# Delta rule with unscaled keys, and its solver's result turned on VectorE, in a two-layer GLA / gated delta / latent attention block

## Chip, cores, metric

One core of a Trainium2 chip runs the whole program. The metric is the device time of one execution in microseconds. Everything is float32.

## What is computed

Two layers work on 512 tokens (256 context, 256 latent) of width 1024. Each layer has three token mixers beside each other: gated linear attention, a gated delta rule in both directions, and latent attention. Only the delta rule is touched. Its definition, cut:

```
def l2norm(x):
    xf = x.astype(jnp.float32)
    return (xf * lax.rsqrt(jnp.sum(xf * xf, axis=-1, keepdims=True) + EPS)).astype(x.dtype)
...
def gdn_chunk_scan(q, k, v, g, beta, s0):
    '''Chunked gated delta rule: S_t = exp(g_t)(I - beta_t k_t k_t^T) S_{t-1} + beta_t k_t v_t^T,
    o_t = q_t S_t. q, k: (B, T, H, DK); v: (B, T, H, DV); g, beta: (B, T, H); s0: (B, H, DK, DV).'''
```

q, k and v come from one projection, a centred convolution of five taps and a SiLU; q and k are then divided by their length over the 128 elements of a head (`l2norm`). Inside a block of tokens the rule needs the inverse of a unit lower triangular matrix L, whose entries below the diagonal are beta times a decay times a product of two keys. There are 8 heads, two directions.

## The kernel before

**Order.** `schedule()` writes one list of items, the plan, such as `("d2", l, g, tt)` for layer l, pair of heads g and token tile tt. `settle()` moves each kind of item by the number of places that the hand-written table `AHEAD` gives it. Each engine then walks the plan from front to end and emits its share of every item; it never passes an item for another. An item waits, through semaphores, for the parts of other engines that it reads, and for the last reader of the PSUM bank that it gets. So the order in the plan is the order on each engine, and a late item holds back everything behind it on that engine. Weights come in over SyncE's queue in units of 1 MB into a ring.

**The delta rule in items.** The heads go in pairs g = 0 to 3. For a pair:
- `dqkv` j = 0 to 5 (q, q, k, k, v, v): projection on TensorE; a ScalarE copy, `cv` with five taps on VectorE (L2124, L2126), SiLU (`dsilu`, `dsil2`; VectorE L2132, L2144).
- `dnq`, `dn` for j = 0 to 3: lengths of q and k. ScalarE squares 128x512 (L1743), TensorE sums over the partitions with a matmul by ONES (bank<-RS,ONES), ScalarE makes the reciprocal root (L1518, L1519), VectorE scales the 512 columns (L2150).
- `d1`, `d2` per token tile: TensorE transposes the summed gates (K,WORK), VectorE makes the decays (L2156, four a tile), TensorE makes k by k and k by q (WORK, 128x128), VectorE multiplies (L2167, L2169, L2170).
- `dd`, `dt` per token tile: ScalarE gathers blocks of 32 x 32 (L1765), VectorE transposes (L2177), SyncE writes the blocks to DRAM (`LD`).
- `sol`: GpSimd loads the blocks (L1104) and the betas (`BD`, L1105) and inverts all 32x32 blocks at once in 31 steps of a multiply and an add (L1114, L1116).
- `dv`: GpSimd writes the result to DRAM (`XD`, L1123) and reads it back in another order (L1129); VectorE copies it (L2199) and transposes four times (L2202).
- `dx`, `dya`, `dyb`, `dx6`, `dy6`: TensorE joins the 32x32 inverses to 128x128 ones by small matmuls; `dx` is the first of them (matmuls of 32x32). Then the scan `sk`, `sq`, `st`, `su`, `sa` runs over the token tiles.

`head(l, g)` is d1, d2, dd, dt of the four tiles and then sol; `invert(l, g)` is dv to dy6. In `gdn()` the pair g = 2 has a placing of its own:

```
            elif g == 2:
                n = len(early) // 2
                out += qk + weave(head(l, 3), early[:n]) + weave(invert(l, g), kv, early[n:])
```

All of head 3 stands ahead of `dv` of pair 2. For g = 0 and 1 the inversion of g is woven with the head of g + 1.

On TensorE all matmuls have one line, L1153 (helper `mm`), and all transposes L1156 (`tr`).

## Time and profile before

| | before |
|---|---|
| median of 3 runs | 2183.26 us (2180.09 to 2183.82) |
| profiled execution, its own time | 2180.62 us |
| span of the trace | 2178.7 us |
| mean granted TensorE clock | 0.991 |
| TensorE busy | 2109.8 us, 97% |
| VectorE busy | 927.1 us, 43% |
| ScalarE busy | 841.6 us, 39% |
| GpSimd busy | 294.7 us, 14% |

The span is that of one execution, which was itself timed with 2180.62 us; what lies around it is 1.9 us. Busy shares are means over the whole program: an engine with a small share can still be the one that is waited for in one place. In the trace a float32 matmul of the program leaves two records.

### The profile page before, as it was taken

How to read it: one execution, taken by the hardware profiler on the slowest of the kernel's cores; microseconds unless marked ns; L12 is line 12 of the kernel's file. 1: busy time of each engine (PE TensorE's matmuls, PEld its weight loads, DVE VectorE, ACT ScalarE, POOL GpSimd, SP SyncE). 2: the span in 40 equal slices, each digit the busy share in tenths (PEclk: the TensorE clock that was granted, in tenths of full speed). 3: DMA queues.
4: the chain of work that ended last, by engine and by line, in shares of the span. 5: the costliest groups of instructions: out<-in, count | busy, mean ns of one | idle time of the engine just before them, and what ended most of it. 6: DMA issues, size and time to landing. Idle time of an engine off the chain costs nothing. (4 is left out here: it accounts for less than half of the span.)

```text
span 2178.7 us, 31299 instructions
## 1 busy us (share of the span) xinstructions
PE 2109.8 (97%) x10890; PEld 1439.6 (66%) x10890; DVE 927.1 (43%) x2293; ACT 841.6 (39%) x2203; POOL 294.7 (14%) x623
## 2 busy tenths in 40 slices
PE   8999999999989999999999999999989979999998
PEld 5667576656556886555674446776676668976687
DVE  3023554857563235443231111246677653343321
ACT  1223354645443234444231112246556443245420
POOL 1000006153350000000000000000632641000000
PEclk9999999999999999999999999999999999999999
DMA  8326303221311022111122332231422312332333
GB/s 271 105 73 195 118 22 109 65 68 43 100 40 49 26 88 79 60 50 44 63 77 78 116 99 101 77 100 41 134 79 74 97 55 78 108 100 85 112 129 122
DMA packets 192443, 192.31 MB, mean 88 GB/s; under 512 B 28943, under 2 KB 186467, under 8 KB 191779
## 3 DMA queue, kind: packets, MB, share of 16 engines
q1 hardware_dynamic: 186048, 171.08, 25.4%
q0 software_dynamic: 4672, 18.89, 2.8%
q8 instruction: 92, 1.51, 0.3%
q10 hardware_dynamic: 1571, 0.34, 0.1%
q14 instruction: 60, 0.49, 0.1%
HBM read 180.78 MB, written 9.50 MB: 87 GB/s over the span
## 5 line engine op out<-in xcount | busy, mean ns | idle before, releaser
L1153 PE MATMUL bank<-hT,ring 128*128 128x512 f32 (+2 forms) x1856 | 715.1, 533 | 5.6 <-ACT hT L1557 3.6
L1153 PEld LDWEIGHTS bank<-hT,ring 128*128 128x128 f32 (+1 forms) x1856 | 331.7, 189 | 257.1 <-issue 239.1
L1153 PE MATMUL bank<-ring,hT 128*128 128x256 f32 (+2 forms) x2112 | 449.8, 368 | 0.0
L1153 PE MATMUL bank<-WORK 128*128 128x128 f32 (+6 forms) x3056 | 392.0, 286 | 37.3 <-DVE O L2202 13.3
L1153 PEld LDWEIGHTS bank<-ring,hT 128*128 128x128 f32 x2112 | 380.4, 190 | 62.4 <-issue 17.2
L1153 PEld LDWEIGHTS bank<-WORK 128*128 128x128 f32 (+4 forms) x3056 | 320.5, 170 | 144.9 <-issue 123.3
L1153 PE MATMUL bank<-yT,ring 128*128 128x512 f32 (+1 forms) x768 | 270.2, 489 | 0.0
L1153 PEld LDWEIGHTS bank<-yT,ring 128*128 128x128 f32 x768 | 139.2, 191 | 78.7 <-issue 69.7
L2126 DVE SCALAR_TENSOR_TENSOR WORK<-WORK,CW 128x512 f32<-128x512 f32 (+1 forms) x192 | 142.1, 740 | 2.2
L1512 ACT ACTIVATE E<-bank 128x512 f32<-128x512 f32 (+1 forms) x84 | 45.0, 536 | 207.4 <-PE bank L1153 198.2
L1116 POOL TENSOR_TENSOR WORK<-WORK 128x126 f32<-128x126 f32 (+22 forms) x248 | 107.3, 432 | 19.4
L1141 POOL DMA_DIRECT2D yT<-xs x2 | 1.1, 547 | 800.7 <-DVE MT L2010 800.7
L1153 PE MATMUL bank<-ring,WORK 128*128 128x384 f32 (+1 forms) x272 | 108.4, 536 | 0.0
L1114 POOL TENSOR_TENSOR WORK<-WORK 128x126 f32<-128x126 f32 (+22 forms) x248 | 100.9, 407 | 19.5
L1156 PEld LDWEIGHTS bank<-K,WORK 128*128 128x128 f32 x634 | 78.3, 142 | 34.8 <-issue 25.2
L1524 ACT ACTIVATE WORK<-bank 128x128 f32<-128x128 f32 (+3 forms) x182 | 47.3, 272 | 135.2 <-PE bank L1153 134.9
L1156 PE MATMUL bank<-K,WORK 128*128 128x128 f32 x634 | 98.3, 279 | 0.2 <-DVE WORK L2314 0.2
L1153 PE MATMUL bank<-MT,ring 128*128 128x512 f32 (+1 forms) x256 | 83.7, 486 | 2.7 <-DVE MT L2010 2.7
L1153 PEld LDWEIGHTS bank<-ring,WORK 128*128 128x128 f32 x272 | 50.1, 190 | 38.0 <-issue 22.7
L1153 PEld LDWEIGHTS bank<-MT,ring 128*128 128x128 f32 x256 | 48.5, 190 | 37.2 <-issue 32.5
L2344 DVE TENSOR_REDUCE WORK<-bank 128x1 f32<-128x512 f32 (+1 forms) x48 | 28.9, 602 | 83.1 <-PE bank L1153 83.1
L1850 ACT ACTIVATE WORK<-bank,WORK 128x512 f32<-128x512 f32 (+1 forms) x48 | 29.6, 616 | 82.6 <-PE bank L1153 52.3
(215 smaller groups left out, 2009.6 us busy)
## 6 DMA issues: line engine op xcount, KB each, us to landing
ring<-in_w_in_dram SPq DMA_DIRECT2D x92, 1024.0 KB, 5.3
ring<-in_w_branch_dram SPq DMA_DIRECT2D x24, 1024.0 KB, 5.1
ring<-in_ada_w_dram SPq DMA_DIRECT2D x18, 1024.0 KB, 7.1
ring<-in_w_out_dram SPq DMA_DIRECT2D x8, 1024.0 KB, 5.1
WORK<-in_ada_w_dram SPq DMA_DIRECT2D x6, 1024.0 KB, 12.6
ring<-in_mla_q_up_dram SPq DMA_DIRECT2D x8, 576.0 KB, 4.1
xs<-yT POOLq DMA_DIRECT2D x2, 2048.0 KB, 7.5
WORK<-LD POOLq DMA_DIRECT2D x16, 256.0 KB, 3.4
```

Source lines behind the costliest of these rows:

```text
L1114: link(pool, "pool", pool.tensor_tensor(t, a[:, j + 1:BASE, j:j + 1].broadcast_to([P, m, w]), y[:, j:j + 1, 0:w].broadcast_to([P, m, w]), ...
L1116: ins = pool.tensor_tensor(y[:, j + 1:BASE, 0:w], y[:, j + 1:BASE, 0:w], t, ALU.subtract)
L1141: pool.dma_start(yT[:, :, :], xs[l]).then_inc(s_back, 16)
L1153: return nc.tensor.matmul(o, a, b, start=start, stop=stop, skip_group_check=True)
L1156: return nc.tensor.transpose(o, a, ident)
L1512: link(act, "act", nc.scalar.activation(dst, src, ACT.Abs))
L1524: ins = nc.scalar.activation(MT2[:, c0:c0 + w], ps[:, c0:c0 + w], ACT.Square, accum_out=mS[:, at + i:at + i + 1])
L1850: ins = nc.scalar.activation(PM[:, s, 0:nk], ps[:, 0:nk], ACT.Exp, bias=MST[:, nth(it, "act") % 8, 0:1], scale=MSCALE, accum_out=MST[:, nt ...
L2126: ins = V_.scalar_tensor_tensor(acc, src, wv, acc, ALU.mult, ALU.add)
L2344: ln(V_.tensor_reduce(MST[:, j, 2:3], ps[:, 0:nk], AX_X, ALU.max))
```

## The change

The keys are no longer divided by their length. `d2` takes the diagonal of k by k, already in PSUM, by a multiply with the identity and a sum over each row (L2145, L2146, VectorE; `KN8`). ScalarE makes reciprocal roots of 128x8 numbers once a pair, and at the last tile's `dt` VectorE works them into the betas (`KB`, turned into the solver's layout `SLB` by one transpose) and into the decays (`EGK`). Where a product still holds an unscaled key, the length is put in as a factor: in `dv` (`KF`, its inverse), and in the PSUM reads of `dx` and `dx6`, which were copies. `dnq` and `dn` remain for q alone. The betas no longer go through TensorE, ScalarE and DRAM (`BT`, `BD`). The solver stores its result with the two block indices exchanged, so that its inner step is 32 elements instead of 1 (a row of the result was contiguous, now a column is), and VectorE turns it by four transposes (L2208) and a multiply (L2210), so that `XD` with its write and its load is gone. The solver's areas are freed by `dv` of the pair before. `AHEAD` has new numbers, and the cut for a pair's early projections now lies at k's SiLU.

```diff
-        XD = nc.dram_tensor("XD", (1, SYSTEMS * BLOCK_D), F32, kind="Internal").ap()
-        BD = nc.dram_tensor("BD", (DEPTH, 4, TT, 4, P), F32, kind="Internal").ap()
...
-                if v[2] < 4:
+                if v[2] < 2:
                     tail += [("dnq",) + v, ("dn",) + v, ("v", "dn") + v]
...
-                n = rest.index(("v", "dn", l, g + 1, 3)) + 1
+                n = rest.index(("v", "dsil2", l, g + 1, 3)) + 1
...
-                    y = SLY[:, 0:BASE * BASE // 2].rearrange("q (i k) -> q i k", i=BASE)
+                    y = SLY[:, 0:BASE * half].rearrange("q (k i) -> q i k", i=BASE)
+                    pool.wait_ge(*done(("dg", l), "dve"))
                     if n:
-                        pool.wait_ge(s_xout, 16 * n)
+                        pool.wait_ge(*done(("dv", (n - 1) // 4, (n - 1) % 4), "dve"))
...
+                    for b in range(NBLK):
+                        pool.dma_start(SLA[b * BASE:(b + 1) * BASE, :], bc(systems(LD)[b:SYSTEMS:NBLK, :], 0, [2, half, BLOCK_D])
+                                       ).then_inc(s_lblk, 16)
+                    pool.wait_ge(s_kbeta, n + 1)
...
-                    pool.dma_start(XD[0, :].rearrange("(q x) -> q x", q=P), SLY[:, 0:BASE * BASE // 2]).then_inc(s_xout, 16)
-                    pool.wait_ge(s_xout, 16 * (n + 1))
...
+                    if tt == TT - 1:
+                        act.wait_ge(s_ksum, TT * (rounds(l, g) + 1))
+                        kn = KN8[:, :, 2 * g:2 * g + 2]
+                        rsqrt(kn, kn, 1.0).then_inc(s_knorm, 1)
...
                 elif k == "d2":
                     _, l, g, tt = it
-                    dve.wait_ge(*done(("d1", l, g, tt), "act"))
...
+                    diag = LTP[:, g % 2, tt, :].rearrange("p (h n) -> p h n", h=2)
+                    ln(V_.tensor_tensor(diag, ps[:, 0:256].rearrange("p (h n) -> p h n", h=2), bc(ident, 1, [P, 2, P]), ALU.mult))
+                    V_.tensor_reduce(KN8[:, tt, 2 * g:2 * g + 2], diag, AX_X, ALU.add).then_inc(s_ksum, 1)
+                    dve.wait_ge(s_ksum, TT * rounds(l, g) + tt + 1)
+                    dve.wait_ge(*done(("d1", l, g, tt), "act"))
...
                 elif k == "dt":
                     _, l, g, tt = it
+                    if tt == TT - 1:
+                        dve.wait_ge(s_knorm, rounds(l, g) + 1)
+                        dve.wait_ge(*done(("dg", l), "act"))
+                        if rounds(l, g):
+                            dve.wait_ge(*done(("sol", (rounds(l, g) - 1) // 4, (rounds(l, g) - 1) % 4), "pool"))
...
+                        V_.transpose(SLB[:, :, :].rearrange("p e i -> p (e i)"), KB[:, :, :, :, :].rearrange("p e o t u -> p (e o t u)")).then_inc(s_kbeta, 1)
...
                 elif k == "dv":
...
+                    ln(V_.reciprocal(KF[:, :, 2:4], KN8[:, :, 2 * g:2 * g + 2]))
...
-                    dve.wait_ge(s_land, 32 * (rounds(l, g) + 1))
-                    link(dve, "dve", V_.tensor_copy(LAND[:, :, :].rearrange("p s (u k h) -> p (s u) k h", k=BASE // 2, h=2),
-                                                    LANDR.rearrange("p (v h k) -> p v k h", h=2, k=BASE // 2)))
+                    dve.wait_ge(*done(("sol", l, g), "pool"))
+                    for b in range(4):
+                        ins = V_.transpose(LANDR[:, b * P:(b + 1) * P], SLY[:, b * P:(b + 1) * P])
+                    ln(ins)
+                    link(dve, "dve", V_.tensor_tensor(LAND[:, :, :].rearrange("p s (u k h) -> p (s u) k h", k=BASE // 2, h=2),
+                                                      LANDR.rearrange("p (k h v) -> p v k h", h=2, k=BASE // 2),
+                                                      KF[:, :, :].rearrange("p t u -> p (t u)").unsqueeze(2).unsqueeze(3).broadcast_to(
+                                                          [P, 4 * TT, BASE // 2, 2]), ALU.mult))
```

The order of the instructions, first on TensorE in layer 0 around the head of pair 3. RS,ONES are the sums of `dn`, hT,ring projections, K,WORK transposes of d1. Before:

```order
L1153 MATMUL bank<-RS,ONES 128x512
L1153 MATMUL bank<-hT,ring 128x512 x8
L1153 MATMUL bank<-RS,ONES 128x512
L1156 MATMUL bank<-K,WORK 128x128 x8
L1153 MATMUL bank<-WORK 128x128 x8
L1156 MATMUL bank<-K,WORK 128x128 x4
L1153 MATMUL bank<-yT,ring 128x512 x2
```

After:

```order
L1136 MATMUL bank<-RS,ONES 128x512
L1136 MATMUL bank<-hT,ring 128x512 x14
L1139 MATMUL bank<-K,WORK 128x128 x8
L1136 MATMUL bank<-WORK 128x128 x8
L1139 MATMUL bank<-K,WORK 128x128 x4
L1136 MATMUL bank<-yT,ring 128x512 x2
```

The last sum of k ahead of the transposes is gone, and the projections stand together; the last of q's remains.

On VectorE, same place, from the third tile's d2 to the end of `dv` of pair 2. Before:

```order
L2167 TENSOR_TENSOR WORK<-bank,SQ 128x512
L2169 TENSOR_TENSOR SQ<-bank,SQ 128x512
L2170 TENSOR_TENSOR WORK<-SQ 128x256
L2006 TENSOR_TENSOR MT<-bank,E 128x512
L2177 STREAM_TRANSPOSE WORK<-WORK 128x64 x2
L2199 COPY WORK<-WORK 128x512
L2202 STREAM_TRANSPOSE O<-WORK 128x128 x4
```

After, from the last tile's d2:

```order
L2145 TENSOR_TENSOR WORK<-bank,K 128x256
L2146 TENSOR_REDUCE WORK<-WORK 128x2
L2152 TENSOR_TENSOR WORK<-bank,SQ 128x512
L2154 TENSOR_TENSOR SQ<-bank,SQ 128x512
L2155 TENSOR_TENSOR WORK<-SQ 128x256
L1988 TENSOR_TENSOR MT<-bank,E 128x512
L2181 STREAM_TRANSPOSE WORK<-WORK 128x64
L2166 TENSOR_TENSOR WORK<-WORK 128x4x2 x2
L2169 TENSOR_TENSOR WORK<-WORK 128x4x2 x2
L2171 COPY WORK<-WORK 128x4x2
L2172 COPY WORK<-WORK 128x2x16
L2173 STREAM_TRANSPOSE WORK<-WORK 128x64
```

and from there to the same transposes:

```order
L2176 TENSOR_TENSOR WORK<-WORK 128x4x2 x2
L2181 STREAM_TRANSPOSE WORK<-WORK 128x64
L2197 RECIPROCAL WORK<-WORK 128x4x2
L2208 STREAM_TRANSPOSE WORK<-WORK 128x128 x4
L2210 TENSOR_TENSOR WORK<-WORK 128x512
L2215 STREAM_TRANSPOSE O<-WORK 128x128 x4
```

Two operations are added to every d2, nine small ones (L2166 to L2176) ahead of the last `dt`, and `dv` has a reciprocal, four transposes and a multiply where it had a copy.

On GpSimd, from one solve's end to the next one's first step. Before:

```order
L1116 TENSOR_TENSOR WORK<-WORK 128x16
L1123 DMA XD<-WORK 128x512
L1129 DMA WORK<-XD 128x16x16 x2
L1098 MEMSET WORK 128x512
L1104 DMA WORK<-LD 64x1024
L1105 DMA WORK<-BD 64x32
L1104 DMA WORK<-LD 64x1024
L1105 DMA WORK<-BD 64x32
L1107 TENSOR_TENSOR WORK<-WORK 128x1024
L1110 COPY WORK<-WORK 64x16 x2
L1114 TENSOR_TENSOR WORK<-WORK 128x31
```

After:

```order
L1111 TENSOR_TENSOR WORK<-WORK 128x16
L1093 MEMSET WORK 128x512
L1098 DMA WORK<-LD 32x1x1024 x4
L1102 TENSOR_TENSOR WORK<-WORK,K 128x16 x2
L1105 TENSOR_TENSOR WORK<-WORK 128x1024
L1109 TENSOR_TENSOR WORK<-WORK 128x31
```

The write and the two loads of XD and the loads of BD are gone; the same 256 KB of L blocks come in four loads instead of two.

## Rows read from the trace of the kernel before

**Rows 1.** The page: busy us (share of the span) and records of each engine

```profile
PE 2109.8 (97%) x10890; PEld 1439.6 (66%) x10890; DVE 927.1 (43%) x2293; ACT 841.6 (39%) x2203; POOL 294.7 (14%) x623
```

**Rows 2.** Windows (us from start): busy time of PE, PEld, DVE, ACT, POOL

```profile
250.00:660.00 410.00, 396.95 (x2241) 253.26 (x2240) 261.19 (x563) 207.93 (x448) 137.64 (x293) 1.00 0.22 63
660.00:1440.00 780.00, 774.83 (x3231) 490.21 (x3233) 231.22 (x641) 243.00 (x724) 7.45 (x13) 1.00 0.22 71
1440.00:1860.00 420.00, 392.67 (x2683) 291.14 (x2684) 262.55 (x612) 216.43 (x500) 139.49 (x294) 0.98 0.29 85
```

**Rows 3.** Waits of TensorE by releaser: us in total, times, longest

```profile
PE bank L1153 <- DVE O L2202: 13.3, 3, 6.2
PE bank L1153 <- DVE WORK L2150: 9.4, 5, 5.5
...
PE bank L1153 <- ACT RS L1743: 2.3, 4, 0.8
```

**Rows 4.** TensorE by form: records, busy us, mean ns

```profile
L1156 PE MATMUL bank<-K,WORK 128*16 128x128 f32 x8 | 1.2, 273 | 0.0
```

**Rows 5.** TensorE, layer 0, head 3 to dx of pair 2: start, length, wait

```profile
592.07 1.02 PE L1153 MATMUL bank<-RS,ONES 128*128 128x512 f32 x2
592.93 1.04 PE L1156 MATMUL bank<-K,WORK 128*128 128x128 f32 x8
595.43 2.02 PE L1153 MATMUL bank<-WORK 128*128 128x128 f32 x16 [1.46 <-DVE WORK L2150]
...
611.15 0.23 PE L1153 MATMUL bank<-WORK 32*32 32x32 f32 x1 [5.45 <-DVE O L2202]
```

**Rows 6.** VectorE, the same place

```profile
594.59 0.69 DVE L2150 SCALAR_TENSOR_TENSOR WORK<-WORK,RS 128x512 f32<-128x512 f32 x1 [2.43 <-ACT RS L1519]
595.20 2.15 DVE L2156 SCALAR_TENSOR_TENSOR SQ<-bank,WORK,K 128x128 f32<-128x128 f32 x8
...
609.47 0.24 DVE L2177 STREAM_TRANSPOSE WORK<-WORK 128x64 f32<-128x64 f32 x1 [0.58 <-ACT WORK L1765]
609.65 0.43 DVE L2199 COPY WORK<-WORK 128x512 f32<-128x512 f32 x1
```

**Rows 7.** TensorE, layer 1: waits at pairs 0, 2 and 3

```profile
1589.26 1.38 PE L1153 MATMUL bank<-WORK 128*128 128x128 f32 x5 [5.46 <-DVE WORK L2150]
...
1762.87 0.23 PE L1153 MATMUL bank<-WORK 32*32 32x32 f32 x1 [6.25 <-DVE O L2202]
...
1811.18 0.18 PE L1153 MATMUL bank<-WORK 32*32 32x32 f32 x1 [1.58 <-DVE O L2202]
```

**Rows 8.** VectorE, layer 1: dv of pair 0, last dt of pair 3

```profile
1587.18 0.43 DVE L2199 COPY WORK<-WORK 128x512 f32<-128x512 f32 x1 [4.40 <-DMA WORK<-XD]
1587.64 0.89 DVE L2202 STREAM_TRANSPOSE O<-WORK 128x128 f32<-128x128 f32 x4
...
1761.19 0.25 DVE L2177 STREAM_TRANSPOSE WORK<-WORK 128x64 f32<-128x64 f32 x1 [0.87 <-ACT WORK L1765]
```

**Rows 9.** GpSimd, layer 1: start and end of the solve of pair 0

```profile
1540.38 1.96 POOL L1107 TENSOR_TENSOR WORK<-WORK 128x1024 f32<-128x1024 f32 x1 [3.09 <-DMA WORK<-BD]
...
1576.84 0.62 POOL L1123 DMA_DIRECT2D XD<-WORK  x1 [0.30 <-POOL WORK L1116]
```

**Rows 10.** VectorE by form: count, busy us, mean ns

```profile
L2006 DVE TENSOR_TENSOR MT<-bank,E 128x256 f32<-128x256 f32 x8 | 3.3, 413 | 3.4 <-PE bank L1153 3.4
L2344 DVE TENSOR_REDUCE WORK<-bank 128x1 f32<-128x256 f32 x16 | 6.8, 423 | 16.9 <-PE bank L1153 16.9
L2041 DVE TENSOR_TENSOR WORK<-WORK 128x4 f32<-128x4 f32 x16 | 2.5, 158 | 0.0
```

**Rows 11.** GpSimd: first multiply by form; one step's add, 1 and 15 columns

```profile
L1107 POOL TENSOR_TENSOR WORK<-WORK 128x1024 f32<-128x1024 f32 x8 | 15.5, 1943 | 27.1 <-DMA WORK<-BD 27.1
345.21 0.26 POOL L1116 TENSOR_TENSOR WORK<-WORK 128x30 f32<-128x30 f32 x1
376.68 0.25 POOL L1116 TENSOR_TENSOR WORK<-WORK 128x30 f32<-128x30 f32 x1
```

More of the change, by code:

```diff
@@ L1026, in _ @@
             todo = [(where[last_use[replaced[u]]] if u in replaced else -1, 0, n, u) for n, u in enumerate(units)]
-            todo += [(where[it], 1, 0, it) for it in plan if it[0] in ("dg", "dt")]
+            todo += [(where[it], 1, 0, it) for it in plan if it[0] == "dt"]
             for at, (_, scratch, _, u) in enumerate(sorted(todo, key=lambda t: t[:3])):
@@ L1101, in _ @@
                         pool.wait_ge(*done(("sol", (n - 1) // 4, (n - 1) % 4), "pool"))
+                    for b in range(NBLK):
+                        pool.dma_start(SLA[b * BASE:(b + 1) * BASE, :], bc(systems(LD)[b:SYSTEMS:NBLK, :], 0, [2, half, BLOCK_D])
+                                       ).then_inc(s_lblk, 16)
+                    pool.wait_ge(s_kbeta, n + 1)
                     for odd in range(2):
[L1103 to L1110 removed]
+                        link(pool, "pool", pool.tensor_tensor(SLY[:, odd:BASE * half:BASE + 2], SLB[:, 1, odd:BASE:2],
+                                                              kc(C_ODD + odd, 1).broadcast_to([P, half]), ALU.mult))
+                    pool.wait_ge(s_lblk, 16 * NBLK * (n + 1))
+                    link(pool, "pool", pool.tensor_tensor(a, a, bc(SLB[:, 0, :], 2, [P, BASE, BASE]), ALU.mult))
                     for j in range(BASE - 1):
@@ L1321, in _ @@
                            GG[:, :, r * BH:(r + 1) * BH])
-                    mm(ps[:, 64:128], ONES[:, :], GG[:, :, :])
-                    for tt in range(TT):
-                        ins = tr(psum(it, 1)[0:16, tt * P:(tt + 1) * P],
-                                 BETA[:, tt, :])
+                    ins = mm(ps[:, 64:128], ONES[:, :], GG[:, :, :])
                 elif k == "dn":
@@ L1349, in _ @@
                     _, l, g, tt = it
-                    for j in (2, 3):
-                        pe.wait_ge(*done(("dn", l, g, j), "dve"))
-                    pe.wait_ge(*done(("dsil2", l, g, 5), "dve"))
+                    for j in range(2, 6):
+                        pe.wait_ge(*done(("dsil2", l, g, j), "dve"))
                     for j in range(4):
@@ L2217, in _ @@
                     _, l, g, n = it
+                    if ("sa", l, g, n - 1) in where:
+                        dve.wait_ge(*done(("sa", l, g, n - 1), "pe"))
                     for u in range(4):
@@ L2249, in _ @@
                         dve.wait_ge(*done(("su", l, g, n - 1), "dve"))
+                        if ("sq", l, g, n) in where:
+                            dve.wait_ge(*done(("sq", l, g, n), "pe"))
                         for u in range(4):
```

113 lines of the change are left out of this document (55 added, 58 removed).

## The prediction

> **What bounds the kernel now.** The page's first part comes first: TensorE is busy 2109.8 of 2178.7 us [rows 1], so nearly all of the time is TensorE's own, and a gain must take work or waits away from it. VectorE has 927.1 us of work, which looks harmless, but the windows show where it lies: in the two delta-rule stretches it is busy 261.19 of 410 us and 262.55 of 420 us, and only 231.22 of 780 us between them [rows 2]. TensorE idles about 13 us in the first of those stretches, 27 in the second and 5 between (window less busy time, same rows). The waits by releaser then say what for: 13.3 us on the transposes of `dv`, in 3 waits; 9.4 us on VectorE's scaling of keys, L2150, in 5; 2.3 us in 4 waits on the squares for lengths [rows 3], which stand, by their starts, at sums of k. These three are the waits that the change touches.
>
> The two timelines side by side show what such a wait is. In layer 0 TensorE starts the transposes for head 3 at 592.93, waits 1.46 us for VectorE's scaling of k, runs out of other work, and waits 5.45 us more until 611.15, where `dx` of pair 2 starts [rows 5]. VectorE meanwhile is not waiting: from 595.20 to 609.65 it works nearly without a gap through the decays of head 3, and only then comes to `dv` of pair 2 [rows 6]. The copy there has no wait before it, so the solver's result had long landed. This stall is VectorE's queue, not the DRAM path. The same stands in layer 1 at 1762.87, 6.25 us [rows 7]. The DRAM path is waited for in one place: layer 1, pair 0. The solver's last add ends at 1576.54 (the write to XD at 1576.84, less its 0.30 of wait [rows 9]), VectorE's copy begins at 1587.18 after 4.40 us idle for XD, its transposes end at 1587.64 + 0.89 = 1588.53 [rows 8]; the scaling of the next keys is queued behind them, and TensorE waits 5.46 us for it [rows 7].
>
> **The change, part by part.** All sums are against the profiled execution, 2180.6 us.
>
> *Lengths of k on TensorE.* 2 keys x 4 pairs x 2 layers = 16 sums by ONES go, all 512 wide (k is needed for all tokens in both layers). One takes from 592.07 to the next instruction's start at 592.93, 0.86 us [rows 5]: 16 x 0.86 = **-13.8**. The busy time of the pair of records is 1.02 us in the same row, but records overlap, so starts decide. Bounds -13 to -15. Their ScalarE and VectorE work (16 x 0.69 us of L2150 = 11.0 us of VectorE [rows 6]) goes too.
>
> *The betas' transposes* go: 8 records, 1.2 us [rows 4], **-1.0** by starts.
>
> *Waits on k's lengths.* The 2.3 us on squares vanish [rows 3]: **-2.3**. Of the 9.4 us in five waits on L2150, 5.46 [rows 7] and 1.46 [rows 5] are dealt with below; three are left with 2.5 us. The product k by k now needs only the SiLU. I take three quarters, as one of the three lies in pair 2's chain of layer 1: **-1.8**.
>
> *Pair 0 of layer 1.* Before: solver's end to the end of the transposes 1588.53 - 1576.54 = 12.0 us. After: four transposes 0.89 [rows 8], a 128x512 multiply 0.69 (as L2150's, with the same two inputs in SBUF [rows 6]), four transposes 0.89, with gaps 2.7. So 9.3 us less. Against it the solver starts later, because its input comes later: the head's four d2 gain 3.34 us (below), nine small operations at 158 ns 1.4, of which about 1.5 fill gaps in VectorE's waiting for ScalarE's gathers (of the kind of 0.58 and 0.87 us [rows 6, 8]): 3.2. And the solver reads with an inner step of 128 bytes. The nearest rows are two adds of 30 elements of one step form: 0.26 us as 30 rows of one element, step 64 bytes, and 0.25 us as two contiguous runs of 15 [rows 11]. 0.01 us in 30 elements, over the 5712 elements of a solve (2856 for each of multiply and add): 1.9 us. Net 9.3 - 3.2 - 1.9 = 4.2 us sooner, while TensorE itself arrives 0.86 sooner, the sum in front of it being gone: 5.46 shrinks by **-3.3**. Bounds: whole (-5.5) if the head's additions hide; nothing if the solver's stride costs 5 us or more.
>
> *Pair 3 of layer 1*: the wait of 1.58 us on `dv` [rows 7] is shorter than the 4.2 us: **-1.6**.
>
> *Pair 2 of both layers.* Here nothing is gained by the shorter path, since the result was there early; the chain that is waited for is VectorE's own, and it grows. Each d2 has a 128x256 multiply from PSUM (413 ns, L2006) and a sum over 128x256 (423 ns, L2344) [rows 10]: 4 x 0.84 = 3.34 us. Nine small ones at 158 ns (128x4, L2041) = 1.4, less the 0.58 and 0.87 us for which VectorE stood idle at that `dt` [rows 6, 8]. `dv` has a reciprocal (0.16), four transposes (0.89 [rows 8]) and a multiply (0.69) for a copy (0.43): 1.3. Together 5.5 in layer 0, 5.2 in layer 1. Against it, the chain starts sooner: before, it began 2.27 us after TensorE's transposes, behind k's scaling (595.20 - 592.93 [rows 5, 6]). Now it waits for the transposes and for the last SiLU of k. But the new order puts k's last projection four projection matmuls nearer to the transposes (some 13 us of TensorE's work ahead instead of 16, at the trace's 0.43 us of start to start for 128x512), so the SiLU comes about as late as it can. I take 0.6 us of start each; bounds 0 and 1.6. **+9.5**; bounds +7.5 to +11. This is the term that speaks against the change: TensorE has the same work in that stretch, so each VectorE microsecond is a TensorE one.
>
> *Other inversions* (pairs 0 and 1, both layers). The same 4.8 us a head and 1.3 us a `dv` fall among convolution taps that have slack of unknown size, and `dx` waits there are small now. VectorE adds in all 8 x (3.34 + 1.4 + 1.3) = 48.6 us less 11.0 = 37.6. Bounds: 0 (hidden behind projections) and 12 (each of four inversions late by half of 6). I take **+4**, nearer to nothing, since these stretches show no `dv` wait now.
>
> *At nothing:* the factors in the reads of `dx` and `dx6` (same width, copy to multiply), new waits of `sk` on the last `sa` and of `su` on `sq` (each reader stands ahead in TensorE's own order), one wider transpose, four loads of L instead of two plus two of betas on GpSimd's queue (it idles between solves), and fewer writes on SyncE's. SyncE's new wait for the solver's loads stands ahead of `dt`; behind it queue the weights, and were they late this would cost, but the loads are through before a solve's first multiply, and a solve lasts 36 us (1540.38 to 1576.54 [rows 9]) ahead of the next one's input. `AHEAD` moves fills about by a few places; the work between the last `dt` and `dx` on TensorE (the order's counts at the trace's durations) comes out within 3 us of before in each pair, so nothing, +-3.
>
> Sum: -13.8 - 1.0 - 2.3 - 1.8 - 3.3 - 1.6 + 9.5 + 4 = **-10.3**, so 2170.3 us. The runs' median lies 2.6 us above the profiled execution (2183.26 to 2180.62): **2173 us**.
>
> **A price that a page has.** The row gives 1.9 us a solve for the step of 128 bytes. The Trainium skill, "GPSIMD Engine Reference", in its section on performance pitfalls for Q7 kernels, says that reading SBUF with a step of over 8 bytes costs about half as much again per element. The trace does not agree for the pair of adds above, 0.26 against 0.25 us, though both are short. By the page's rule, worked with the row of 1943 ns for 1024 elements [rows 11], it would be 0.95 ns x 5712 = 5.4 us a solve, the gain at pair 0 of layer 1 would vanish, and the sum be about -7.
>
> **The rivals.**
>
> *A, the additions hide.* For it: VectorE is at 63% in these stretches [rows 2], and the chain may start 1.6 us sooner and find d2 waiting for ScalarE's exponentials anyway, so that the diagonal costs nothing (it is put ahead of that wait). Against: in rows 6 VectorE has no gap between 595.20 and 609. Then pair 2 costs +3 and the rest 0: -24 + 3 = -21, median about 2162. Chance 0.20.
>
> *B, VectorE's load eats the gain.* 37.6 us more work, and if 60% of it lands on TensorE (22.6 us in place of 13.5), the sum is -1, median 2182. For it: late taps are late keys, which are a late next head. Against: the stretches' waits are few. Chance 0.16.
>
> *C, the other side: the solver with its step is slow.* If a solve takes x us more than the 1.9, `dv` is late in turn: pair 0 of layer 1 at once, the others once their slack is gone, for which I choose 5, 8 and 13 us (in those pairs no `dv` wait stands in rows 7, so some slack is there, and none is as tight as this one): cost x + (x-5) + (x-8) + (x-13), each where positive. It cancels the 10.3 at x = 7.7 and is past no change by 4.4 us at x = 9.3, a solver of some 47 us in place of 36. For it: no row has an inner step of 128 bytes with a long inner run. Against: the 64-byte row. Chance 0.10: time 2188 to 2200. The page's rule (x = 3.5) belongs to the forecast's range.
>
> **Numbers.** Forecast 0.50, its own range 2166 to 2179; A 0.20, 2159 to 2165; B 0.16, 2179 to 2187; C 0.10; 0.04 for a larger gain. Leaving out C and the far end of A, the range is 2161 to 2185. What this measurement tells from no change is 0.2%, 4.4 us: 2178.9 to 2187.6. Faster 0.48 + 0.20 + 0.04 + 0.01 of B = 0.73; same 0.02 + 0.14 = 0.16; slower 0.10 + 0.01 = 0.11.
>
> **What would show it.** RS,ONES with 16 fewer matmuls, TensorE's busy time 14 to 15 us lower. Before pair 2's `dx` in layer 0 waits of 6.9 + 4.9 = 11.8 us in all, where they were 1.46 and 5.45; in layer 1 about 6.25 + 4.6 = 10.9 (A: no more than 8 in each). In VectorE's rows L2145 and L2146 at 0.41 and 0.42 us, 32 each. Layer 1, pair 0: wait 1 to 3 us. GpSimd's adds within 5% of before; wrong if they take half as much again. The forecast fails if the scattered waits on `cv` or SiLU grow, which I sized by choice.

## The result, and the profile after

| | before | after |
|---|---|---|
| median | 2182.79 us (5 runs) | 2189.88 us (5 runs, 2188.56 to 2191.79) |
| ratio | | 1.0037 (95%: 1.0025 to 1.0048) |
| span of the trace | 2178.7 us | 2187.3 us |
| mean granted clock | 0.991 | 0.985 |

I had forecast 2173 us, within 2161 to 2185, and gave "slower" a chance of 0.11. The kernel became 7.1 us slower: outside the range, and slower where I had forecast faster.

The page of the changed kernel, span and busy time (answers to [rows 1]):

```profile
span 2187.3 us, 31284 instructions
PE 2096.4 (96%) x10850; PEld 1436.4 (66%) x10850; DVE 962.9 (44%) x2455; ACT 816.8 (37%) x2169; POOL 307.6 (14%) x599
```

TensorE's work did go: 13.4 us less busy time. VectorE has 35.8 us more, as the sum had it (37.6). So TensorE stands idle 90.9 us where it was 68.9. The waits of TensorE by releaser say for what (answers to [rows 3]; "issue" is a wait for which the profile names no releaser):

```profile
PE bank L1136 <- DVE O L2215: 32.1, 6, 11.4
PE bank L1136 <- issue: 7.8, 6, 3.1
...
PE bank L1136 <- DVE WORK L2274: 4.8, 5, 1.3
PE bank L1136 <- DVE WORK L2219: 3.7, 3, 2.2
```

L2215 are the transposes at the end of `dv`: 13.3 us in 3 waits are now 32.1 in 6. The waits on the scaling and the squares of k (9.4 and 2.3 us) are gone as forecast. L2274 is VectorE's part of `su` in the scan, L2219 its read of `dx`. Leaving out the waits on `dv`, and in the kernel before also the 11.7 us on the lengths of k, TensorE's idle time rose from 43.9 to 58.8 us. These 14.9 us are waits for which my sum had no term. The timeline of TensorE has the large ones (answers to [rows 5, 7]):

```profile
398.61 0.18 PE L1136 MATMUL bank<-WORK 32*32 32x32 f32 x1 [2.50 <-DVE O L2215]
609.84 0.23 PE L1136 MATMUL bank<-WORK 32*32 32x32 f32 x1 [11.39 <-DVE O L2215]
1581.00 1.03 PE L1136 MATMUL bank<-WORK 128*128 128x128 f32 x4 [2.04 <-DVE WORK L2126]
1588.29 0.23 PE L1136 MATMUL bank<-WORK 32*32 32x32 f32 x1 [6.27 <-DVE O L2215]
1670.55 0.18 PE L1136 MATMUL bank<-WORK 32*32 32x32 f32 x1 [0.98 <-DVE O L2215]
1696.48 1.36 PE L1136 MATMUL bank<-WORK 128*128 128x128 f32 x8 [3.07 <-issue]
1772.98 0.23 PE L1136 MATMUL bank<-WORK 32*32 32x32 f32 x1 [10.17 <-DVE O L2215]
```

L2126 is the product of a SiLU on VectorE, here that of k. Pair 2 waits 11.39 and 10.17 us, where the prediction said 11.8 and 10.9. That term is right. Pair 0 of layer 1 waits 2.04 + 6.27 us, where the prediction said 2.2 in all.

For pair 0 of layer 1, GpSimd's rows show why. Start of the loads, first multiply, and on VectorE the first transpose of the result:

```profile
1536.87 2.38 POOL L1098 DMA_DIRECT2D WORK<-LD  x4 [18.26 <-issue]
1546.08 2.02 POOL L1105 TENSOR_TENSOR WORK<-WORK 128x1024 f32<-128x1024 f32 x1 [5.84 <-DMA WORK<-LD]
1585.29 0.89 DVE L2208 STREAM_TRANSPOSE WORK<-WORK 128x128 f32<-128x128 f32 x4 [3.52 <-POOL WORK L1111]
```

The first multiply began at 1540.38 before [rows 9]; it is 5.7 us later. Of that 1.6 us is the first issue (1536.87 against 1535.23, each on its own run's clock) and 4.1 us the load: 9.2 us from the first issue instead of 5.2. In the quieter second solve of layer 0 the load takes 8.5 us; these are the rows of the kernel before, then of the one after:

```profile
430.12 0.55 POOL L1104 DMA_DIRECT2D WORK<-LD  x1 [44.17 <-issue]
435.06 1.91 POOL L1107 TENSOR_TENSOR WORK<-WORK 128x1024 f32<-128x1024 f32 x1 [2.83 <-DMA WORK<-BD]
```

```profile
424.91 2.39 POOL L1098 DMA_DIRECT2D WORK<-LD  x4 [25.80 <-DMA LD<-WORK]
433.43 1.91 POOL L1105 TENSOR_TENSOR WORK<-WORK 128x1024 f32<-128x1024 f32 x1 [5.57 <-DMA WORK<-LD]
```

The steps of the solve themselves, by line, all 248 of each; before, then after:

```profile
L1116 POOL TENSOR_TENSOR WORK<-WORK 128x126 f32<-128x126 f32 (+22 forms) x248 | 107.3, 432 | 19.4
L1114 POOL TENSOR_TENSOR WORK<-WORK 128x126 f32<-128x126 f32 (+22 forms) x248 | 100.9, 407 | 19.5
```

```profile
L1109 POOL TENSOR_TENSOR WORK<-WORK 128x126 f32<-128x126 f32 (+22 forms) x248 | 121.4, 490 | 19.4
L1111 POOL TENSOR_TENSOR WORK<-WORK 128x126 f32<-128x126 f32 (+22 forms) x248 | 120.4, 485 | 19.4
```

33.6 us more in 8 solves, 4.2 us each; I had taken 1.9. The adds take 12% more, where the prediction named 5% as its sign, and the multiplies 20% more.

**The clock.** The windows around pair 2 of layer 0; first the kernel before, then after (columns as in [rows 2]; the value ahead of the DMA share is the granted clock):

```profile
606.00:612.00 6.00, 0.85 (x62) 0.88 (x64) 4.96 (x14) 3.77 (x12) 0.00 (x0) 0.90 0.14 22
612.00:618.00 6.00, 6.00 (x143) 4.17 (x134) 2.72 (x7) 1.87 (x6) 2.52 (x5) 0.81 0.38 96
```

```profile
598.00:604.00 6.00, 0.45 (x2) 0.00 (x0) 5.76 (x14) 3.00 (x8) 0.00 (x0) 0.80 0.08 12
604.00:610.00 6.00, 0.16 (x12) 0.20 (x16) 5.72 (x26) 1.89 (x6) 0.19 (x1) 0.50 0.15 23
610.00:616.00 6.00, 6.00 (x105) 3.40 (x101) 1.51 (x4) 1.76 (x5) 3.21 (x7) 0.57 0.26 72
```

While TensorE stands, its granted clock falls to 0.50, that is from 2.4 to 1.2 GHz, and TensorE's next work runs at 0.57 of full speed for 6 us: 2.6 us lost on top of the wait. In the kernel before it was 1.1 us in the window behind the wait (0.81). The same loss, TensorE's busy time times what its clock lacks of 1, is 16.3 us over the whole of the execution before and 19.6 after. Idle time is 68.9 and 90.9 us, and so work at full clock 2093.5 and 2076.8. That adds up: 16.7 us of work less, 22.0 of idle more and 3.3 of slow clock more are the 8.6 us between the two spans. The sum had 14.8 us of work less, and no term for the clock.

The 3.3 us are not pair 2's alone. Its two falls cost 5.8 us together before and 7.5 after. Four smaller ones are new, of 1.7 us each, behind waits of 1.7 to 3.1 us; this is one, behind the 3.07 us at 1696.48, where TensorE is busy all the time:

```profile
1697.00:1701.00 4.00, 4.00 (x19) 3.64 (x18) 1.66 (x4) 2.19 (x4) 1.32 (x4) 0.57 0.77 211
```

Against them stand smaller losses elsewhere, most of it in the first 60 us (4.8 us before, 1.6 after), long before the delta rule begins. So how much slow clock belongs to the change isn't sharp: 3.3 us over everything, 6.3 from 60 us on (11.3 to 17.6, by windows of 2 us).

**Where the idle time lies.** I cut both traces at the starts of `dx`. TensorE's idle time grew by 6.7 and 8.0 us in the stretches that end at pair 2's `dx` (6.9 to 13.6 in layer 0, 9.2 to 17.2 in layer 1), by 1.1 and 5.2 in those that end at pair 1's, and by 2.6 between layer 0's pair 3 and layer 1's pair 0. Of the 14.7 us ahead of pair 2, 8.4 are the two large waits (with the 1.46 before them counted in the kernel before); the rest, 4.1 us of it in layer 1, is in smaller waits, the 3.07 us at 1696.48 and 2.23 us for the read of `dx` among them.

### The profile page after: what moved, and what is told of

The parts are those of the page before. It is cut to its first block, busy times and chain, and to the rows that moved or that the text cites. A ratio compares the mean times of both kernels' runs of the same rounds, so it can differ in the third digit from the quotient of the medians.

```text
span 2187.3 us, 31284 instructions
## 1 busy us (share of the span) xinstructions
PE 2096.4 (96%) x10850; PEld 1436.4 (66%) x10850; DVE 962.9 (44%) x2455; ACT 816.8 (37%) x2169; POOL 307.6 (14%) x599
## 3 DMA queue, kind: packets, MB, share of 16 engines
q0 software_dynamic: 10176, 14.59, 2.0%
## 4 chain that ended last, share of the span: by engine, by line
PE 85%; DVE 5%; POOL 3%; issue 3%; ACT 2%; DMA 1%; ACTq 0%; DVEq 0%; SPq 0%; POOLq 0%
PE bank L1136 82%; PE bank L1139 3%; POOL WORK L1109 1%; POOL WORK L1111 1%; DVE SQ L2137 1%; DMA WORK<-LD 1%; DVE WORK L2108 0%; DVE SQ L2154 0%; DMA ring<-in_ada_w_dram 0%; DVE WORK L2210 0%; DVE WORK L2208 0%; DVE WORK L2152 0%; DVE WORK L2146 0%; DVE WORK L2145 0%; ACT WORK L1747 0%
## 5 line engine op out<-in xcount | busy, mean ns | idle before, releaser
L1136 PE MATMUL bank<-WORK 128*128 128x128 f32 (+6 forms) x3056 | 393.9, 287 | 55.0 <-DVE O L2215 32.1
L1136 PEld LDWEIGHTS bank<-ring,hT 128*128 128x128 f32 x2112 | 380.5, 190 | 62.5 <-issue 16.7
L1109 POOL TENSOR_TENSOR WORK<-WORK 128x126 f32<-128x126 f32 (+22 forms) x248 | 121.4, 490 | 19.4
L1111 POOL TENSOR_TENSOR WORK<-WORK 128x126 f32<-128x126 f32 (+22 forms) x248 | 120.4, 485 | 19.4
L2010 DVE SCALAR_TENSOR_TENSOR WORK<-bank,WORK 128x512 f32<-128x512 f32 x16 | 11.1, 692 | 119.8 <-ACT WORK L1493 119.8
```

The lines of the kernel that those rows point to most:

```text
L1109: link(pool, "pool", pool.tensor_tensor(t, a[:, j + 1:BASE, j:j + 1].broadcast_to([P, m, w]), y[:, j:j + 1, 0:w].broadcast_to([P, m, w]), ...
L1111: ins = pool.tensor_tensor(y[:, j + 1:BASE, 0:w], y[:, j + 1:BASE, 0:w], t, ALU.subtract)
L1136: return nc.tensor.matmul(o, a, b, start=start, stop=stop, skip_group_check=True)
L2010: ins = V_.scalar_tensor_tensor(LA[:, tt, :], ps[:, :], 0.0, LT1, ALU.min, ALU.subtract)
```

## The experiments

Two theories at the start. **S**: the solver's result comes late (slower loads, slower steps) and that is the loss. **V**: VectorE's additions are the loss. `nodiag` and `nokn` leave out work that the result needs. The ratios are to the kernel before, timed beside each run. The changed kernel was timed in one session, so "faster than the changed kernel" compares medians of different sessions, in which the kernel before moved between 2181.66 and 2182.79 us: I don't tell differences of under 2 us apart.

**rows**: the result row by row again, read with a step by the transposes.

```diff
-                    y = SLY[:, 0:BASE * half].rearrange("q (k i) -> q i k", i=BASE)
+                    y = SLY[:, 0:BASE * half].rearrange("q (i k) -> q i k", i=BASE)
...
-                        ins = V_.transpose(LANDR[:, b * P:(b + 1) * P], SLY[:, b * P:(b + 1) * P])
+                        ins = V_.transpose(LANDR[:, b * P:(b + 1) * P].rearrange("p (k v) -> p k v", v=BASE),
+                                           SLY[:, 0:BASE * BASE // 2].rearrange("p (i k) -> p k i", i=BASE)[:, 4 * b:4 * b + 4, :])
```

> The changed kernel, but the solver keeps its result row by row (inner step 1 element, as before) and VectorE's four transposes read it with a step. Theory S (the loss is the solver's result coming late: slower loads and slower steps): a solve falls back by 3 to 4 us to about 33 us, the wait before dx of pair 0 in layer 1 falls from 6.3 to about 3 us, those of 2.5, 1.0 and 0.8 us go, the two waits of pair 2 (11.4 and 10.2 us) stay, and the time falls by 5 to 8 us against the changed kernel, ratio to before 1.000 to 1.0015. Theory V (VectorE's additions for the diagonal alone make the loss): under 2 us, ratio 1.003 to 1.004. VectorE's transposes with a step may cost more than 0.89 us; at twice that 1 us is given back.

Measured: 2186.37 us, ratio 1.0024 (1.0014 to 1.0033), 3.5 us faster than the changed kernel. Steps and transposes by line:

```profile
L1111 POOL TENSOR_TENSOR WORK<-WORK 128x126 f32<-128x126 f32 (+22 forms) x248 | 107.2, 432 | 19.4
L1109 POOL TENSOR_TENSOR WORK<-WORK 128x126 f32<-128x126 f32 (+22 forms) x248 | 104.8, 423 | 19.4
L2208 DVE STREAM_TRANSPOSE WORK<-WORK 128x128 f32<-128x128 f32 x32 | 9.6, 359 | 1.8 <-POOL WORK L1111 1.6
```

241.8 us of steps became 212.0: the inner step of 128 bytes costs 29.8 / 8 = 3.7 us a solve, 0.65 ns an element. The transposes pay 0.3 us a solve. The wait ahead of pair 0's `dx` in layer 1 is shorter, but 5.0 us and not the 3 that S gave, with 0.80 on L2126 where it was 2.04:

```profile
1586.71 0.23 PE L1136 MATMUL bank<-WORK 32*32 32x32 f32 x1 [4.98 <-DVE O L2216]
```

The waits of 2.50 and 0.98 us, which S said would go, are 2.76 and 1.31: longer by what the transposes pay, so there it is VectorE's own chain that is late, not the solver's result. Pair 2 waits 11.70 and 10.50 us. The time lies between the two theories' numbers. The slower step carries up to half of the loss (3.5 of 7.1 us, or 2.8 if each kernel is taken against the kernel before of its own session); the slower loads are not in it.

**load8**: eight loads of 16 rows in place of four that each copy 16 rows twice.

```diff
-                    for b in range(NBLK):
-                        pool.dma_start(SLA[b * BASE:(b + 1) * BASE, :], bc(systems(LD)[b:SYSTEMS:NBLK, :], 0, [2, half, BLOCK_D])
-                                       ).then_inc(s_lblk, 16)
+                    for b in range(2 * NBLK):
+                        pool.dma_start(SLA[b * half:(b + 1) * half, :], systems(LD)[b // 2:SYSTEMS:NBLK, :]).then_inc(s_lblk, 16)
```

> The changed kernel with eight loads of 16 rows for the blocks of L in place of four loads that each copy 16 rows twice. If the copying twice in one load is what cuts them into packets of 512 bytes, GpSimd's queue shows packets of 4 KB again (some 130 instead of 1088 per solve) and the time from the first issue to the first multiply is 8 issues of 0.6 us and then 2.9, 7.7 us, against 8.5 now and 5.0 before. If the rows' distance in DRAM is what cuts them, it stays over 8.5.

GpSimd's queue over the whole program, in the changed kernel, then here (packets, MB, share of 16 engines):

```profile
q0 software_dynamic: 10176, 14.59, 2.0%
```

```profile
q0 software_dynamic: 3520, 14.56, 2.0%
```

The same bytes in a third of the packets: the double copy in one load is what cut the rows. A solve's loads are 256 packets instead of 1088, twice the 130 that I had expected. The load now takes 6.4 us in layer 0's second solve (426.95 to 433.31), 2.1 less than in the changed kernel and less than the 7.7 expected. The kernel was executed once, with 2193.84 us, and pair 0 of layer 1 waits 6.18 us there, as in the changed kernel (6.27). One execution can't tell 2 us, so what the faster load is worth stays open.

**nodiag**: the diagonal's product and sum left out, the lengths a constant.

```diff
-                    ln(V_.tensor_tensor(diag, ps[:, 0:256].rearrange("p (h n) -> p h n", h=2), bc(ident, 1, [P, 2, P]), ALU.mult))
-                    V_.tensor_reduce(KN8[:, tt, 2 * g:2 * g + 2], diag, AX_X, ALU.add).then_inc(s_ksum, 1)
+                    V_.memset(KN8[:, tt, 2 * g:2 * g + 2], 1e4).then_inc(s_ksum, 1)
```

> The changed kernel without the diagonal: the multiply with the identity and the row sum in d2 are left out and the lengths set to a constant. Theory V: 4 x 0.84 = 3.3 us less at each head, 11.4 and 10.2 at pair 2 become about 8 and 7, and with pair 0 and 1 the time falls by 8 to 12 us, ratio to before about 0.999. Theory S: pair 2 gives 6.7 us and the clock some more, pair 0 of layer 1 gives up to 3 because the solver starts sooner: also 8 to 10 us. What tells them apart is where: under S the wait at pair 0 of layer 1 stays above 2 us.

Measured: 2170.01 us, ratio 0.995 (0.9938 to 0.9963), 19.9 us faster than the changed kernel. More than either theory had. The 26.7 us of VectorE work cost 19.9. (The constant that stands in their place takes 1.9 us of VectorE; from one start to the next a tile's part shrinks from 0.90 to 0.11 us, 25 us in all.) TensorE's waits:

```profile
PE bank L1136 <- DVE O L2213: 24.1, 5, 8.3
PE bank L1136 <- issue: 6.3, 8, 1.6
```

The time from one pair's dx to the next one's shrinks in layer 1 by 8.0 us ahead of pair 2, 2.0 ahead of pair 1, and 2.6 us between layer 0's pair 3 and layer 1's pair 0; in layer 0 by 5.8 and 1.5. It isn't pair 2 alone, though 13.8 of the 19.9 us are ahead of its `dx`, where four of the eight heads lie, with 13.4 us of diagonal; the two large waits shrink by 5.3. Between the two profiled executions, 14.4 us of idle time went, 8.0 of it on `dv` and 6.4 elsewhere, and 2.1 us of slow clock.

What was to tell the theories apart does not speak for V alone. At pair 0 of layer 1 the wait stays above S's 2 us, with 1.65 us on L2126 ahead of it:

```profile
1581.62 0.23 PE L1136 MATMUL bank<-WORK 32*32 32x32 f32 x1 [4.44 <-DVE O L2213]
```

So at that place the later result is a cause of its own, beside the diagonal.

**nokn**: the kernel before, k's lengths cut to 8 of 512 columns.

```diff
-                    a0 = q0 if it[3] < 2 else 0
+                    a0 = q0 if it[3] < 2 else T - 8
                     ins = mm(ps[:, a0:T], ONES[:, :], bSQ[:, a0:T])
```

> The kernel before, with the lengths of k cut from 512 to 8 columns (squares, sum, root and scaling of the other 504 left out; all SiLU products scaled by 0.01), nothing put in their place. This is the gain side of the change alone. My prediction's terms: 13.8 less a rest for 8 columns (16 x about 0.1), 2.3 and 1.8 of waits, and pair 2's waits of 6.9 shorter by about 0.6 each: 17 us, about 2165, ratio 0.992. If the removed work had been hidden or its place taken by other waits (theory H), under 8 us, ratio above 0.9965.

Measured: 2166.3 us, ratio 0.9931 (0.9918 to 0.9945), 15.7 us faster than before. The gain side of the forecast holds. Theory H falls. So what the change adds costs 2189.9 - 2166.3 = 23.6 us, net of what its shorter path to `dx` and its new order gain, and the diagonal with 19.9 is most of it.

**accum**: two multiplies that sum as they write, per tile.

```diff
-                    ln(V_.tensor_tensor(diag, ps[:, 0:256].rearrange("p (h n) -> p h n", h=2), bc(ident, 1, [P, 2, P]), ALU.mult))
-                    V_.tensor_reduce(KN8[:, tt, 2 * g:2 * g + 2], diag, AX_X, ALU.add).then_inc(s_ksum, 1)
+                    V_.scalar_tensor_tensor(diag[:, 0, :], ps[:, 0:P], 1.0, ident, ALU.mult, ALU.mult,
+                                            accum_out=KN8[:, tt, 2 * g:2 * g + 1])
...
```

> The changed kernel, with the diagonal's multiply and sum (128x256 each, 0.41 + 0.42 us) done by two 128x128 multiplies that sum as they write. Theory V2 (VectorE sets the pace of the heads' stretches, and some three quarters of its added time shows: 26.7 us of diagonal gave 19.9 us): at 0.27 us each (the multiplies of 128x128 by form) 32 x 0.3 = 9.6 us of VectorE less, time 6 to 8 us less, about 2183, ratio 1.000. Theory P2 (only the chain in front of pair 2's dx counts, the rest hides): 2 x 1.2 = 2.4 us less, ratio 1.0025. If the summing form is slower than 0.27 us, less of both.

Measured: 2181.25 us, ratio 1.0003 (0.9994 to 1.0011), 8.6 us faster. By form a multiply takes 0.28 us and the reading of its sum 0.08 more:

```profile
L2147 DVE SCALAR_TENSOR_TENSOR WORK<-bank,K 128x128 f32<-128x128 f32 x32 | 9.1, 284 | 0.0
L2147 DVE DVE_READ_ACCUMULATOR WORK<-bank,K 128x1 f32 x32 | 2.6, 82 | 0.0
```

By these records the diagonal's own work is 23.3 us instead of 26.7, and the time fell by more than that. But the records overlap. From the first start to the start of the next operation it is 0.90 us in the changed kernel and 0.54 here; first the changed kernel:

```profile
599.10 0.41 DVE L2145 TENSOR_TENSOR WORK<-bank,K 128x256 f32<-128x256 f32 x1
...
600.00 0.69 DVE L2152 TENSOR_TENSOR WORK<-bank,SQ 128x512 f32<-128x512 f32 x1
```

```profile
595.62 0.28 DVE L2145 SCALAR_TENSOR_TENSOR WORK<-bank,K 128x128 f32<-128x128 f32 x1
...
596.16 0.69 DVE L2154 TENSOR_TENSOR WORK<-bank,SQ 128x512 f32<-128x512 f32 x1
```

At 32 tiles that is 11.5 us of VectorE's queue less, and 8.6 us of time (7.5 if each kernel is taken against the kernel before of its own session) is 65 to 75% of it, near nodiag's 79% by the same count (19.9 of 25). P2 with its 2.4 us falls; V2 holds.

**oldorder**: seven numbers of AHEAD back to those of before.

```diff
-AHEAD = {... 'yT': 2, 'muk': -2, 'muq': 5, 'z2': 4, 'sk': 2, 'dsilu': 2, 'su': 1 ...}
+AHEAD = {... 'yT': -1, 'muk': -6, 'muq': 2, 'z2': -4, 'sk': -1, 'dsilu': -2 ...}
```

> The changed kernel with seven of the fifteen changed numbers of the order table set back to before's (sk, su, yT, z2, muk, muq, dsilu). Theory O (the new order is part of the loss: su behind sk's wait shows 1.3 us waits that were 0.4): 3 us or more faster, ratio 1.002 or less. Theory V2: the order was made for the changed kernel and moves little, within 2 us, or slower.

Measured: 2200.04 us, ratio 1.008 (1.0066 to 1.0094), 10.2 us slower. Theory O falls: the new numbers are worth 10 us to the changed kernel. What they would do to the kernel before was not tried.

**woven2**: pair 2 woven as pairs 0 and 1.

```diff
-                out += qk + weave(head(l, 3), early[:n]) + weave(invert(l, g), kv, early[n:])
+                out += qk + weave(weave(invert(l, g), kv), head(l, 3), early, phase=(-1.0,))
```

> The changed kernel with the inversion of pair 2 woven with the head of pair 3, as it is for pairs 0 and 1, in place of behind it. Theory P2: the waits of 11.4 and 10.2 us before dx of pair 2 fall under 2 us each, some of it comes back as waits inside the inversion, net 8 us or more faster, and the two falls of the granted clock (0.5 for 5 to 10 us) go: ratio under 1.000. Theory V2: the waits go from dx to the pieces of the head and to k by k, since VectorE has the same work in that stretch: 0 to 5 us faster from the clock and from the better filling. The solve of pair 3 starts later by some 3 us, which has to fit in the 9 us between its end and dx of pair 3.

Measured: 2203.31 us, ratio 1.010 (1.0086 to 1.0114), 13.4 us slower; both theories wrong in sign. The waits ahead of pair 2's dx are gone, and these stand ahead of pair 3's, in layers 0 and 1:

```profile
668.06 0.23 PE L1136 MATMUL bank<-WORK 32*32 32x32 f32 x1 [10.98 <-DVE O L2215]
1833.91 0.23 PE L1136 MATMUL bank<-WORK 32*32 32x32 f32 x1 [14.96 <-DVE O L2215]
```

The solve of pair 3 began at 629.50 in layer 0 where it was 618.50, 11 us later and not the 3 I had reckoned, and ended some 3 us ahead of that dx. Three microseconds are what `dv` takes, so it is now the solve that this `dx` waits for. P2, by which only the chain ahead of pair 2 counts, falls: the wait at pair 2 is the price of an early solve of pair 3.

**rows_acc_woven**: those three edits together.

> The changed kernel with three things: result stored row by row (-3.5 us alone), diagonal by summing multiplies, pair 2 woven. If they add: V2 gives -3.5 - 7 - 0 to 5, 2175 to 2179, ratio 0.996 to 0.998, faster than before; P2 gives -3.5 - 2.4 - 8 = 2176.

Measured: 2186.76 us, ratio 1.0026 (1.0017 to 1.0035). 3.5 + 8.6 - 13.4 would be 1.3 us slower than the changed kernel; it is 3.1 faster. They don't simply add.

**late**: the diagonal read once a head out of the 32x32 blocks that ScalarE gathers, where the decay is 1; the roots behind the last gather instead of ahead of it, the betas two items later. The two operations in each `d2` are gone; of the edit, this is what takes their place.

```diff
+                        cut = DC[:, 1, 0:TT * 2 * BASE].rearrange("p (t u i) -> p t u i", t=TT, u=2)
+                        ln(V_.tensor_tensor(cut, STG[:, :, 0:2 * BASE].rearrange("p t (u i) -> p t u i", u=2),
+                                            kc(C_SUM, 32).unsqueeze(1).unsqueeze(1).broadcast_to([P, TT, 2, BASE]), ALU.mult))
+                        V_.tensor_reduce(KN8[:, :, 2 * g:2 * g + 2], cut, AX_X, ALU.add).then_inc(s_ksum, 1)
+                        pending = [l, g, 0]
...
```

> The changed kernel, but the lengths are read from the 32x32 diagonal blocks that ScalarE has gathered anyway: once a head a 128x256 multiply and a 128x256 sum behind the last gather, in place of four of each in d2, and the nine small operations on the betas come two items later, while the solver's input is loading. The decay on the diagonal is 1, so the numbers are the same. VectorE loses 26.7 - 6.7 = 20 us. Theory V2 (three quarters of VectorE's time in these stretches shows): 15 us faster than the changed kernel, about 2175, ratio 0.996 to 0.9975. Theory S (the solver's lateness is what is left): under 8 us, ratio above 1.000. The betas must not come later than the load (7.9 to 9.2 us), or the solver waits for them.

Measured: 2182.28 us, ratio 1.0001 (0.9992 to 1.001), 7.6 us faster, half of what V2 said. ScalarE's timeline in layer 1, pair 2, shows waits that may hold the rest (the last row is the copy for the scan's first step):

```profile
1682.68 0.30 ACT L1498 ACTIVATE WORK<-WORK,EPSC 128x8 f32<-128x8 f32 x1 [1.86 <-DVE WORK L2191]
...
1684.30 0.58 ACT L1697 ACTIVATE WORK<-bank 128x512 f32<-128x512 f32 x1
...
1688.76 0.63 ACT L1711 ACTIVATE WORK<-WORK 128x512 f32<-128x512 f32 x1 [2.04 <-DVE WORK L2142]
1689.30 0.58 ACT L1789 ACTIVATE WORK<-bank 128x512 f32<-128x512 f32 x1
```

ScalarE waits 1.86 us for the sum, VectorE then 2.26 us for ScalarE's copy of v's projection (L1697), ScalarE 2.04 us for VectorE's SiLU, and TensorE stands 4.42 us, put down to issue; I take it to be for the scan's copy at the end of that queue. The first of these waits is new. In the changed kernel the roots stand ahead of the last gather, and their sums are there already:

```profile
1688.15 0.30 ACT L1497 ACTIVATE WORK<-WORK,EPSC 128x8 f32<-128x8 f32 x1
```

**late_rows**: late and rows.

> The same with the solver's result stored row by row (-3.5 us alone). If the two add, 2171, ratio 0.994 to 0.996; if the solver's lateness no longer matters once the heads are early (or matters more), the difference to the run above is 0 (or 5).

Measured: 2179.41 us, ratio 0.9987 (0.9978 to 0.9996). They add to 0.6 us.

**late_rows_dv**: and `dv` of pair 2 ahead of head 3.

```diff
+                out += qk + [("dv", l, g)] + weave(head(l, 3), early[:n]) + weave(invert(l, g)[1:], kv, early[n:])
```

> The same with dv of pair 2 placed ahead of the head of pair 3, and dx to dy6 where they were. The solver's result is there some 35 us before, so VectorE can turn it in a gap ahead of the head: 2.9 us less in each of the two chains that TensorE waits for, and a shorter fall of the clock: 4 to 7 us faster than without it. If VectorE has no gap there, no change.

Measured: 2181.3 us, ratio 0.9994 (0.9986 to 1.0003); no gain, 1.9 us slower by the medians. The wait moved from `dx` to its successor, for VectorE's read of `dx` (18.3 us in 3, the longest 8.8). The transposes of `dv` were only the place of the wait, not its cause.

**late2_rows**: late_rows with the roots two items later on ScalarE, the betas four on VectorE.

```diff
-LAG = 2
+LAG = 4
+ALAG = 2
...
+                if roots:
+                    roots[2] += 1
+                    if roots[2] > ALAG or (k in ("dd", "sol") and it[2] != roots[1]):
```

> As late_rows, but ScalarE takes the reciprocal roots two items after the last gather and VectorE the betas four items later, so that neither stands waiting for the other in front of v's convolution and of the scan's first copy. Theory Q (ScalarE's and VectorE's hand-over in the head's tail costs 1.9 and 2.3 us of standing in layer 1, pair 2, and the like elsewhere): 3 to 6 us faster than late_rows, 2174 to 2177. If the tail is VectorE's work and not its waits: no change.

Measured: 2169.45 us, ratio **0.9944** (0.9931 to 0.9958): 12.3 us faster than the kernel before, 20.4 faster than the changed one. It is 10.0 us faster than late_rows, where Q had 3 to 6. Between the two profiled executions TensorE's idle time fell by 5.8 us (80.5 to 74.7), which is Q's size, and the loss by slow clock by 7.7 (22.9 to 15.3), which Q had not; 3.1 of the latter lie in the first 60 us, where the edit does nothing. ScalarE in the same place:

```profile
1674.59 0.30 ACT L1499 ACTIVATE WORK<-WORK,EPSC 128x8 f32<-128x8 f32 x1
...
1677.73 0.63 ACT L1721 ACTIVATE WORK<-WORK 128x512 f32<-128x512 f32 x1 [0.76 <-DVE WORK L2150]
1678.27 0.58 ACT L1797 ACTIVATE WORK<-bank 128x512 f32<-128x512 f32 x1
```

The roots no longer wait. TensorE's waits put down to issue fall from 12.8 in late_rows to 5.9 us, those on `dv` stay (24.2 there):

```profile
PE bank L1138 <- DVE O L2235: 24.5, 5, 8.6
PE bank L1138 <- issue: 5.9, 6, 2.1
```

**late2_rows_st**: and `st` two places earlier (`'st': 2`).

> The same with the item st (the scan's first product and ScalarE's copy of it) two places earlier in the order, ahead of a SiLU of v. The waits of 3.8 and 4.5 us put down to issue fall; 2 to 5 us more. If st moves ahead of its inputs instead, the wait only moves, or others grow: 0 or slower.

Measured: 2170.39 us, ratio 0.9952 (0.9939 to 0.9964). No gain.

**st2**: the changed kernel with `'st': 2` alone.

> The changed kernel with st two places earlier and nothing else. If the queue on ScalarE in front of the scan is a part of the loss that stands alone, waits of 2.5 and 3.1 us fall and it is 2 to 4 us faster, ratio 1.002; if it is only a place where VectorE's lateness shows, under 1 us.

Measured: 2190.76 us, ratio 1.0045 (1.0032 to 1.0058). No gain: the queue ahead of the scan is where lateness shows, not its source.

**cut**: the changed kernel with v's last projection ahead of the head.

```diff
-                n = rest.index(("v", "dsil2", l, g + 1, 3)) + 1
+                n = rest.index(("dqkv", l, g + 1, 5)) + 1
```

> The changed kernel with the cut of a pair's early projections behind the last projection of v, as it was in the kernel before, in place of behind k's SiLU. The head starts 0.9 us of projection later, and v's last projection is ahead of it. Theory C (the new cut puts v's convolution into the scan and costs the waits there): 2 us or more faster. Theory V2: no change, within 1.5 us, or slower.

Measured: 2194.04 us, ratio 1.006 (1.0047 to 1.0072), 4.2 us slower. Theory C falls.

## Why the prediction was wrong

- **The step that failed: what VectorE's added work costs outside the two waits of pair 2.** The sum had +4 for the other inversions, chosen near to nothing "since these stretches show no `dv` wait now", and the scan and the read of `dx` at nothing. The missing wait shows that VectorE was in time, not by how much. The +4 itself came out as the `dv` waits that it named (2.50 at pair 0 of layer 0, 0.98 at pair 1 of layer 1). What had no term are the 14.9 us of other idle time, 2.3 of them waits for a SiLU's product (L2126), the kind that the prediction's last sentence named. nodiag takes away 26.7 us of VectorE's work and gains 19.9, in five of the stretches between one `dx` and the next. That is rival B's mechanism: VectorE's load lands on TensorE. B had 60% of the load; the diagonal shows 75%. B's cost of 22.6 us is near the 23.6 between nokn and the changed kernel; its sum still counted 5.9 us for pair 0, pair 3 and the betas, most of which did not come. (The load in the prediction, 48.6, is 48.3 by its own terms.)
- **Lengths of k, and their waits: right.** -13.8, -2.3, -1.8 and part of pair 2 were forecast as about 17 us; nokn measured 15.7.
- **Pair 2, +9.5: right in its mechanism and its idle time** (11.39 and 10.17 us against 11.8 and 10.9, +8.4 in place of +9.5). The term had only the wait. The slower clock in and behind these two waits cost 1.7 us more than before, and 3.3 us over the program. No part of the sum had it.
- **Pair 0 of layer 1, -3.3, and pair 3, -1.6: wrong.** The shorter path is real: from the start of the transposes to `dx` it is 1588.29 - 1585.29 = 3.0 us, where 12.0 us lay between the solver's end and the last transpose. But "four loads of L instead of two" stood under "at nothing". They cost 3.6 to 4.1 us per solve, 2.1 of them by the small packets (load8), and the steps of the solve cost 4.2 instead of 1.9. So the 4.2 us sooner were used up: the last transposes end at 1588.15 where they ended at 1588.53, each on its own run's clock. TensorE, with less to do, comes to that wait earlier (1582.0 against 1583.8), so in place of -3.3 the wait grew from 5.46 to 8.3 us in all. Pair 3's wait fell only to 0.76 us.
- **The Trainium skill's rule against the row.** "GPSIMD Engine Reference", performance pitfalls, has about half as much again per element beyond 8 bytes of step. rows measures 0.65 ns an element, where the page's rule gave 0.95 by my estimate and the two adds of 30 elements 0.33. Neither is right; the measured one lies between. Two adds of 0.26 and 0.25 us differ by one unit of what the trace prints, too little to size a step from.
- **Order at nothing, +-3: not shown, and too narrow.** Seven of the numbers are worth 10.2 us to the changed kernel (oldorder), and the place of the cut 4.2 (cut). Whether they would have helped the kernel before as much is open.
- **Rival C** had the right place and sign. The solver with its load is some 8 us later per solve than before, that is x of about 6 over the 1.9. By C's own formula this costs 7 us of the 10.3, so it leaves a gain, and the step's 3.7 us alone gave back 3.5 us of time (rows).

What stays open: what the load's 2 us are worth, and what makes up the rest of the 14.9 us. nodiag takes back 6.4 of them; the read of `dx` with its factor, the work on the betas and the new waits in the scan were not tried alone.
